# A mixture-of-experts loop: TensorE's work grouped by tile shape, a VectorE signal behind the further passes, and the first quarter of gate/up loaded ahead of the down weights

## What is computed

```python
gu = xe @ w_gu[eid] + b_gu[eid]            # [tokens, 1024] @ [1024, 2048]
g, u = jnp.split(gu, 2, axis=-1)
g = jnp.minimum(g, SWIGLU_LIMIT)
u = jnp.clip(u, -SWIGLU_LIMIT, SWIGLU_LIMIT)
act = (u + 1.0) * (g * jax.nn.sigmoid(SWIGLU_ALPHA * g))
y = act @ w_down[eid] + b_down[eid]        # [tokens, 1024] @ [1024, 1024]
# out[token] += gate[token, expert] * y
```

## Time and profile before

| | us |
|---|---|
| timed runs: median (lowest, highest) | 1322.68 (1320.38, 1326.93) |
| profiled execution, device time | 1322.67 |
| its span in the trace | 1320.9 |
| TensorE matmul busy | 1264.1 (96%) |
| VectorE busy | 551.6 (42%) |
| ScalarE busy | 178.1 (13%) |
| DMA, mean over the span | 362 GB/s |

### The profile page before, as it was taken

One profiled execution on the slowest core, in us unless ns is written; L12 is line 12 of the kernel. 1 busy time (PEld: TensorE's weight loads), 2 busy tenths in 40 slices (PEclk: granted clock), 3 DMA queues, 4 the chain that ended last, 5 costly groups with the idle time before them and its releaser, 6 DMA issues.

```text
span 1320.9 us, 16859 instructions
## 1 busy us (share of the span) xinstructions
PE 1264.1 (96%) x5957; PEld 582.7 (44%) x5958; DVE 551.6 (42%) x1232; ACT 178.1 (13%) x378; POOL 12.6 (1%) x31
## 2 busy tenths in 40 slices
PE   5999999999999999999899999999999999899997
PEld 4867867788653333333333333333333333233332
DVE  3344686332254344433433443334344343334344
ACT  2102323330020110001100000001000111001002
POOL 0000000110000000000000000000000000000000
PEclk9999999999999999999999999999999999999999
DMA  9967666337659999999999999999999999799994
GB/s 355 326 230 280 237 208 205 115 128 305 255 217 410 428 429 429 429 429 428 428 428 428 429 429 428 429 429 427 404 429 429 429 427 428 294 430 429 429 429 209
DMA packets 59182, 477.53 MB, mean 362 GB/s; under 512 B 4991, under 2 KB 5076, under 8 KB 32532
## 3 DMA queue, kind: packets, MB, share of 16 engines
q1 hardware_dynamic: 58852, 476.11, 87.6%
q10 hardware_dynamic: 304, 1.06, 0.2%
HBM read 476.10 MB, written 1.05 MB: 361 GB/s over the span
## 4 chain that ended last, share of the span: by engine, by line
PE 74%; DMA 18%; DVE 5%; issue 2%; ACT 1%; DVEq 0%; ACTq 0%; SPq 0%
PE bank L1737 24%; DMA down_ring<-in_w_down 17%; PE bank L1776 15%; PE bank L1373 11%; PE bank L1563 4%; PE bank L1725 3%; PE bank L1703 3%; PE bank L1462 2%; PE bank L1408 2%; PE bank L1619 2%; PE bank L1695 2%; DVE scratch L1208 1%; DVE scratch L1206 1%; DMA xres<-in_x 1%; PE bank L1806 1%
## 5 line engine op out<-in xcount | busy, mean ns | idle before, releaser
L1737 PE MATMUL bank<-gu_ring,scratch 128*64 128x512 f32 x2048 | 459.3, 595 | 0.4 <-DVE scratch L1133 0.4
L1737 PEld LDWEIGHTS bank<-gu_ring,scratch 128*64 128x64 f32 x2048 | 143.5, 137 | 283.2 <-issue 282.9
L1776 PE MATMUL bank<-down_ring,scratch 128*64 128x512 f32 x1024 | 235.5, 602 | 24.1 <-DMA down_ring<-in_w_down 18.8
L1373 PE MATMUL bank<-gu_ring 128*128 128x256 f32 x640 | 143.8, 381 | 0.0
L1776 PEld LDWEIGHTS bank<-down_ring,scratch 128*64 128x64 f32 x1024 | 71.2, 137 | 146.3 <-issue 133.5
L1373 PEld LDWEIGHTS bank<-gu_ring 128*128 128x128 f32 x640 | 119.8, 190 | 20.3 <-issue 4.0
L1196 DVE TENSOR_TENSOR scratch<-bank,bgu 128x512 f32<-128x512 f32 x32 | 22.1, 691 | 219.1 <-PE bank L1703 219.1
L734 ACT ACTIVATE scratch<-bank 128x512 f32<-128x512 f32 x32 | 19.1, 597 | 686.1 <-PE bank L1737 686.1
L1164 DVE TENSOR_TENSOR xres<-xres,bank 128x512 f32<-128x512 f32 x132 | 81.9, 682 | 57.6 <-PE bank L1725 57.6
L1703 PEld LDWEIGHTS bank<-ident,scratch 128*128 128x128 f32 x392 | 41.1, 140 | 80.2 <-issue 26.7
L1132 DVE TENSOR_TENSOR scratch<-bank,a 128x256 f32<-128x256 f32 x66 | 27.8, 421 | 115.0 <-PE bank L1703 115.0
(11 more groups left out here) (271 smaller groups left out, 841.4 us busy)
## 6 DMA issues: line engine op xcount, KB each, us to landing
gu_ring<-in_w_gu SPq DMA_DIRECT2D x128, 2048.0 KB, 24.1
down_ring<-in_w_down SPq DMA_DIRECT2D x64, 2048.0 KB, 17.3
gu_ring<-in_w_in SPq DMA_DIRECT2D x32, 1024.0 KB, 8.9
gu_ring<-in_w_ada SPq DMA_DIRECT2D x16, 1024.0 KB, 7.0
down_ring<-in_w_ada SPq DMA_DIRECT2D x8, 512.0 KB, 10.7
gu_ring<-in_w_ada SPq DMA_DIRECT2D x8, 512.0 KB, 11.7
gu_ring<-in_w_pa SPq DMA_DIRECT2D x4, 1024.0 KB, 6.4
gu_ring<-in_w_pb SPq DMA_DIRECT2D x4, 1024.0 KB, 6.2
```

The source lines that it names most:

```text
L1373: last = M(dst[:, b * T:(b + 1) * T], group_chunk(group, kt // 4)[:, kt % 4, cols], hT[:, kt, :], start=kt == 0, stop=kt == KT - 1)
L1737: last = M(bank[f // 2][64 * a:64 * a + 64, :], xT[:, kt % 4, kt // 4, :], gu_ring[:, 8 * half + kt, f * 512:(f + 1) * 512], start=kt == 0 ...
L1776: last = M(bank[7][64 * a:64 * a + 64, :], act_sb[:, kt % 4, kt // 4, :], down_ring[:, kt // 2, (kt % 2) * D + a * 512:(kt % 2) * D + (a + ...
```

## The change

On TensorE, `give(item - 1)` moves from within the gate/up product to between the further passes and the down product. `take` is done in one piece, ahead of the transposes of u. `take_transposed` moves from the middle of the down product to behind `way_back`. give writes banks 0, 1, 2 and 4 in place of 4 to 7. Within the loop it also waits for a new semaphore, `passes_over`, which VectorE counts up by a one-column memset behind its own branch round the further passes. `add_given` stands behind `take` on VectorE instead of ahead of the activation, and the gate/up product waits at its head until it is done (with a memset ahead of the loop that makes the count one higher). On ScalarE `copy_back` moves behind the further passes and waits for give. A further pass uses banks 1 and 3 where it used 5 and 6. On SyncE, from item 19 on, the first quarter of the next expert's gate/up is loaded ahead of the down weights, and the other three behind them.

```diff
@@ load order (SyncE)
-            for step in range(4):
+            for step in range(3):
...
-            load_item_down(TOGETHER + 4)
-            load_item_gu(TOGETHER + 5, 1)
-            load_item_down(TOGETHER + 5)
-            with sp.Fori(TOGETHER // 2 + 3, PAIRS) as n:
+            def load_after_first(item, half):
+
+                load_gu_pair(item + 1, half, 0)
+                load_item_down(item)
+                for j in range(1, 4):
+                    load_gu_pair(item + 1, half, j)
+
+            load_after_first(TOGETHER + 3, 0)
+            with sp.Fori(TOGETHER // 2 + 2, PAIRS - 1) as n:
                 for half in range(2):
-                    load_item_gu(n * 2 + half, half)
-                    load_item_down(n * 2 + half)
+                    load_after_first(n * 2 + half, 1 - half)
+            load_after_first(NE - 2, 1)
+            load_item_down(NE - 1)
@@ ScalarE
             def copy_back(item):
 
                 act.wait_ge(back_done, item + 2)
+                if not isinstance(item, int):
+                    act.wait_ge(given_done, item * 4 + 4)
...
+                further_passes(act, item, count, further)
                 copy_back(item)
-                further_passes(act, item, count, further)
@@ VectorE
             take(0)
+            V.memset(small[:, 4:5], 0.0).then_inc(given_added, 1)
...
                 pick(item + 1)
-                add_given(item - 1)
...
                 further_passes(dve, item, count, lambda b, k: further(item, b, k))
+                V.memset(small[:, 5:6], 0.0).then_inc(passes_over, 1)
                 take(item + 1)
+                add_given(item - 1)
@@ TensorE
                 pe.wait_ge(y_ready, item + 2)
                 pe.wait_ge(back_ready, item + 2)
+                if not isinstance(item, int):
+                    pe.wait_ge(passes_over, item + 2)
...
                 pe.wait_ge(xTe_ready, item + 1)
+                pe.wait_ge(given_added, item * 4 + 1)
...
-                    if kt == 1:
-                        give(item - 1)
...
-                pe.wait_ge(given_added, item * 4 + 4)
-                take(item + 1, (0,))
+                take(item + 1)
                 pe.wait_ge(raw_ready, item * 2 + 2)
                 transposes(3, u_raw).then_inc(uT_done, 1)
-                take(item + 1, (1,))
                 way_back(item)
+                take_transposed(item + 1)
                 further_passes(pe, item, count, lambda b, k: further(item, half, fills, k))
+                give(item - 1)
                 for kt in range(KT):
-                    if kt == KT // 2:
-                        take_transposed(item + 1)
```

More of the change, by code:

```diff
@@ L324, in build @@
         f_mark = sem("f_mark")
+        passes_over = sem("passes_over")
         out_ready = sem("out_ready")
@@ L378, in build @@
         TURN_G2B = 42
+        GIVEN = (0, 1, 2, 4)
         EMPTIED_HT = KT
@@ L747, in further @@
                 act.wait_ge(f_back_done, k + 1)
-                A(f_back, bank[5][:, 0:T], ACT.Copy).then_inc(f_back_ready, 1)
+                A(f_back, bank[1][:, 0:T], ACT.Copy).then_inc(f_back_ready, 1)
                 act.wait_ge(f_gu_done, k + 2)
@@ L768, in _ @@
                 tt, half = n // 2, slice(n % 2 * 512, (n % 2 + 1) * 512)
-                act.wait_ge(given_added, NE * 4 + n + 1)
+                act.wait_ge(given_added, NE * 4 + n + 2)
                 A(xn[:, 1, half] if tt else scratch[:, half], xres[:, tt, half], ACT.Square, accum_out=osq[:, n:n + 1]
@@ L1163, in add_given @@
                     dve.wait_ge(given_done, item * 4 + (n + 5))
-                    V.tensor_tensor(xres[:, tt, cols], xres[:, tt, cols], bank[4 + n][:, :], ALU.add
+                    V.tensor_tensor(xres[:, tt, cols], xres[:, tt, cols], bank[GIVEN[n]][:, :], ALU.add
                                     ).then_inc(given_added, 1)
@@ L1230, in by_quarters @@
                     return t.rearrange("p (q c) -> p c q", c=2).unsqueeze(3).to_broadcast([P, 2, 4, FCAP])
-                taken = bank[6][:, 0:KT * FCAP].rearrange("p (c q s) -> p c q s", c=2, q=4)
+                taken = bank[3][:, 0:KT * FCAP].rearrange("p (c q s) -> p c q s", c=2, q=4)
                 raw = bank[2][:, :].rearrange("p (j f s) -> p j f s", j=4, f=4)
@@ L1724, in give @@
                     rows_ = slice(64 * a, 64 * a + 64)
-                    M(bank[4 + n][:, :], back[rows_, tt * P:(tt + 1) * P], y_sb[rows_, :], start=True, stop=True
+                    M(bank[GIVEN[n]][:, :], back[rows_, tt * P:(tt + 1) * P], y_sb[rows_, :], start=True, stop=True
                       ).then_inc(given_done, 1)
@@ L1791, in further @@
                 last.then_inc(f_taken, 1)
+                pe.wait_ge(f_mark, k + 1)
                 pe.wait_ge(f_gated, (expert + k) * 2 + 2)
-                pe.wait_ge(back_ready, expert + 2)
+                pe.wait_ge(raw_ready, expert * 2 + 2)
                 for tt in range(TT):
-                    last = nc.tensor.transpose(bank[5][:, tt * P:(tt + 1) * P],
+                    last = nc.tensor.transpose(bank[1][:, tt * P:(tt + 1) * P],
                                                f_gates[:, tt, :, :].rearrange("p a s -> p (a s)"), ident[:])
@@ L1798, in further @@
                 pe.wait_ge(f_xraw, k + 1)
+                pe.wait_ge(act_ready, expert * 2 + 2)
                 for c in range(2):
-                    last = nc.tensor.transpose(bank[6][:, c * P:(c + 1) * P], f_x[:, c * P:(c + 1) * P], ident[:])
+                    last = nc.tensor.transpose(bank[3][:, c * P:(c + 1) * P], f_x[:, c * P:(c + 1) * P], ident[:])
                 last.then_inc(f_takenT, 1)
-                pe.wait_ge(f_mark, k + 1)
                 pe.wait_ge(f_xT_ready, k + 1)
```

## The result

| | before | after |
|---|---|---|
| timed and profiled runs, median (lowest, highest), us | 1323.14 (1320.38, 1326.93) | 1382.49 (1377.32, 1385.02) |
| profiled execution, us | 1322.67 | 1377.32 |
| its mean granted TensorE clock | 0.996 | 0.970 |

The ratio is 1.0448 with a 95% interval of 1.0423 to 1.0472: the change costs 59 us, where 20 were forecast. The other three executions of the changed kernel had a mean clock of 0.964 to 0.967 and took 5 to 8 us more than the profiled one.

What follows compares the result with a forecast made beforehand. Bound: TensorE's cycle in experts 16 to 31, loads some microseconds behind. Expert 31's down product starts 20.4 later, the tail saves 0.6: 1322.67 + 20.4 - 0.6 = 1342.5 us; range 1334 to 1351, chance 0.79.

Steps and rivals of the forecast that it cites:

- The direction: Whole kernel: slower, chance 0.87; same 0.09, faster 0.04.
- the wait: TensorE ahead of give, waiting for VectorE's memset behind its activation and branch: 1.79 us of each cycle.
- The quick cycle: TensorE per expert without a further pass: 28.60 us, 1.23 more than the 27.37 before.
- the pass: The only further pass, in expert 25: costs 23.8 us, against 23.5 before.
- S(0): Start of expert 0's down product: moves from 409.99 to 412.0.
- rival 4: TensorE's clock falls in the new gaps ahead of give; no size given, chance next to nothing.
- the last give: give on TensorE, moved to right ahead of the down product: 1.91 us.
- start of expert 31's down product: Near the loop's end: 1322.4, which is 20.4 later than 1301.98.
- the tail: Behind the start of expert 31's down product: no transposes inside down, -0.6 us; the rest unchanged.
- 2 (the signal costs more): VectorE's branch or its return adds 0.4 us an expert, 12.4 more, total 1355; chance 0.08.
- 3: Loads set the pace anyway, so the change does not slow; chance with the hidden-wait rival 0.13.
- 1: Wait ahead of give hidden, saved shape changes decide: cycle 26.81, total 1319; chance with the loads-set-the-pace rival 0.13.

## Why the prediction was right or wrong

**The direction and the wait were right.** The quick cycle is 28.51 where 28.60 was worked out, and the gap ahead of give 1.95 where 1.79 was. The cycle's terms hold one by one: 21.39 for 21.41 up to take, 1.82 for 1.87 of take, 3.38 for 3.41 from the transposes of u to give, 1.92 for 1.91 of give. Loads bind nowhere; waits for down_ring are gone; DMA idles longer in and behind the pass, all as foretold. S(0) came at 412.5 for 412.0.

**The step that failed is rival 4.** I wrote that the stretch of 606 to 871 "had gaps of 1.4 to 1.9 at each expert with the granted clock at 1.00" and gave a fall of the clock next to nothing. That was two errors in reading. First, the stretch ends at 871.00, 0.7 us behind the end of the one gap of 1.9, so what followed that gap lies outside it; up to 875 the mean is 0.99. Second, those gaps were not of one kind: eight experts had 1.4 and 0.7, one had 1.9. The kernel before, at expert 15 and at 16, which the earlier trace rows quote in part, in TensorE's timeline:

```profile
835.98 3.65 PE L1776 MATMUL bank<-down_ring,scratch 128*64 128x512 f32 x16 [1.37 <-DMA down_ring<-in_w_down]
839.56 0.66 PE L1703 MATMUL bank<-ident,scratch 128*128 128x128 f32 x4
840.96 3.65 PE L1776 MATMUL bank<-down_ring,scratch 128*64 128x512 f32 x16 [0.74 <-DMA down_ring<-in_w_down]
...
870.32 5.35 PE L1776 MATMUL bank<-down_ring,scratch 128*64 128x512 f32 x16 [1.92 <-DMA down_ring<-in_w_down]
```

And the granted clock behind the first and the last of these gaps:

```profile
836.00:839.30 3.30, 3.30 (x16) 1.03 (x16) 0.00 (x0) 0.00 (x0) 0.00 (x0) 1.00 1.00 427
...
870.30:873.60 3.30, 3.28 (x9) 1.16 (x11) 0.00 (x0) 0.00 (x0) 0.00 (x0) 0.53 0.98 417
```

The waits of 1.37 and 0.74 with work between them left the clock alone. The gap of 1.92, as long as the one I forecast, had a clock of 0.53 behind it, and expert 16's second half of the down product took 5.35 in place of 3.65: 1.70 us. The pass has a second place of the kind:

```profile
1128.66 5.34 PE L1819 MATMUL bank<-down_ring,scratch 128*32 128x512 f32 x32 [2.62 <-DVE scratch L1248]
```

The window of 1129.60 to 1133.00 behind it had a granted clock of 0.55, and the run with eight unread products takes 3.64 for these 32 instructions behind the same 2.62. The third line of the earlier trace rows, 0.95 over 33 us, is that fall; I used it for the DMA alone. The earlier trace rows had the first: six instructions in 2.67 at 870.32 and in 1.51 at 835.98. I used that row for the date of the last wait and did not compare its busy time. Priced from it, with every cycle hit, rival 4 would have been 30 x 1.70 = 51 us on top of 1342.5; the runs show two cycles in three, 34 us.

The Trainium skill has this as a loop whose waits for loads throttle the clock again at each tile ("TensorE: Matmul & The Clock Gate", HAM oscillation). In its example the waits are longer than the products between them; here 1.95 us stand idle in a cycle of 28. Our trace agrees that a fall can come back from turn to turn of a loop, though not with every one here: ten of 30 cycles were spared. Why those ten, with the same gap, stays open. So does how sure the fall behind 1.92 was: the kernel before with the new load order has the same gap at the same place, at 871.93, and 3.65 behind it.

**The terms, against the profiled execution.** What TensorE's rows give, as differences from the forecast:

| term | forecast | measured | difference |
|---|---|---|---|
| start of expert 0's down product | 412.0 | 412.5 | +0.5 |
| 30 cycles without the clock | 28.60 | 28.505 | -2.9 |
| the clock, in 20 of them | 0 | 1.64 each, one 2.7 | +34.0 |
| the pass | 23.8 | 25.6 | +1.8 |
| the last give | 1.91 | 2.84 | +0.9 |
| start of expert 31's down product | 1322.4 | 1356.6 | +34.2 |

With 0.6 in the tail that is the 34.8 between 1342.5 and 1377.32. The median lies 5 us higher still, in executions with a lower mean clock, which have no trace here. The changed kernel with the load order of before has one of that kind, 1381.35 at 0.967: its 30 cycles add up to the same, but its loop begins 1.4 later and its pass takes 56.7 from give to give instead of 54.1. So the 5 us can stand outside the 30 cycles; for the changed kernel itself that is not shown.

**The pass was mis-sized by VectorE's branches.** I took 0.9 from TensorE's gap of kind "issue" at 1137.74; VectorE's took 2.25, which is 1.35 of the 1.8; the rest was not traced. The price of another engine's branches was not the price of this one's. The pass's forecast also held a fall of the clock without my seeing it, since 27.6 was read from a pass with one inside. The profiled execution with eight unread products had no fall there, and its pass took 23.9 where the changed kernel's took 25.6. That is the luck in its total: longer branches and a spared fall cancelled, and 1342.2 came out for 1342.5. The Trainium skill ("Advanced Engine Details and Errata", Control Flow Timing) gives a compare-and-branch 108 ns. The 2.25 here is the closing of a loop with its registers and branches, some twenty times that: the trace has eight compare-and-branches of 0.05 to 0.07 us each there, and register steps and pauses between them.

**Rivals.** 2 (the signal costs more) fell: 1.95 of gap, hardly more than forecast, and the quick cycle below it. 3 fell, as no load binds. 1's mechanism is what the kernel without the wait shows: own cycle 26.48, loads bind. Its price, 1319, was missed by 7 us. Three differences make them: gate/up's last quarter of expert 25 let TensorE go on at 1108.7 and not at 1104; from there the down product followed after 38.2 us, not 34.2; and the six quicker cycles behind it gave back 1.8. From the end of gate/up to the down product the pass took 33.0 us in that kernel and 30.0 in the first run with give ahead of the branch.

**The range** was made from the bounds of the wait alone. Its error was not its width but that the one rival that decided had no price in it.

## What to carry to other kernels

A wait on TensorE costs its own length and what the clock does behind it. Here that was 34 us on top of the 20 that the change costs without it. Look for an old gap of the same length, and compare the busy time of the row right behind it with the same row elsewhere. The mean clock of a long stretch shows a fall that comes back each cycle (0.96 above), but hides a single one. A signal that only a rare pass needs belongs into that pass, or the work that needs it ahead of the branch; here the second was the cheaper, 1320.3 against 1326.1. If a gap can't be closed, split it or put cheap products in it: eight unread products an expert gave back 40 us, though that kernel was still 20 us slower than before.

## What the runs showed of the hardware

- Idle time of TensorE in one piece: 1.06 behind unread products, 1.37 behind transposes and 1.51 inside a gate/up product left the granted clock, or the pace of what followed, as it was. Behind gaps of 1.92, 1.95 and 2.54 the next 3.3 us had 0.50 to 0.59, at 1.3 to 1.7 us a time.
- The length alone doesn't decide: gaps of 1.95 were spared in ten cycles of 30, gaps of 2.54 in ten of 31, one of 2.09 where one of 2.02 was hit, and one of 2.68 in one execution where its like of 2.69 was hit in the other.
- Five changes of tile shape fewer and 0.19 less of waiting take the cycle from 27.37 to 26.48, so a change costs about (0.89 - 0.19) / 5 = 0.14 us, if all of the rest is theirs.
- The end of a loop of further passes holds VectorE for 2.25 us. It holds TensorE for 0.86, and for 3.1 where TensorE waits for VectorE right ahead of it.
